# The prompt's cross attention, worked head by head between the chunk products of the query projection

## What is computed

```python
def cross_attend(xn, mk, mv, w_xq, w_xo):
    B, L = xn.shape[:2]
    q = (xn @ w_xq).reshape(B, L, N_X_HEADS, X_HEAD_DIM)
    s = jnp.einsum('bqhd,bkhd->bhqk', q, mk.astype(q.dtype)).astype(F32) * (X_HEAD_DIM ** -0.5)
    p = jax.nn.softmax(s, axis=-1).astype(q.dtype)
    o = jnp.einsum('bhqk,bkhd->bqhd', p, mv.astype(q.dtype))
    return o.reshape(B, L, X_WIDTH) @ w_xo
```

## Time and profile before

| | us |
|---|---|
| median of 3 runs | 1618.1 |
| lowest and highest | 1615.92, 1622.6 |
| the profiled execution | 1617.97 |
| its span | 1616.2 |

### The profile page before, as it was taken

How to read it: one execution, slowest core, us unless ns; L and a number is a source line. 1 busy time by engine, 2 the same in 40 slices (tenths; PEclk the granted TensorE clock), 3 DMA queues, 4 the chain that set the end, 5 groups by cost and what they waited for, 6 DMA issues and landing times.

```text
span 1616.2 us, 25068 instructions
## 1 busy us (share of the span) xinstructions
PE 1533.8 (95%) x9990; PEld 1474.5 (91%) x9990; DVE 647.3 (40%) x1187; ACT 444.2 (27%) x803; POOL 241.6 (15%) x269
## 2 busy tenths in 40 slices
PE   7999999888799899889999999999999999999997
PEld 6999888787699898778898999999999999999997
DVE  5544666454545421333356332233222432233322
ACT  6422444233221110332134320133111321033212
POOL 2100000232265300122442000000000000000143
PEclk9999999899599999999999999999999999999999
DMA  7553100102231211025542111111111111111112
GB/s 209 186 181 96 38 27 14 50 27 83 93 95 52 92 39 39 1 104 171 175 138 65 53 39 52 40 53 39 52 42 50 40 52 52 40 46 46 50 29 108
DMA packets 153774, 115.43 MB, mean 71 GB/s; under 512 B 13904, under 2 KB 143120, under 8 KB 153424
## 3 DMA queue, kind: packets, MB, share of 16 engines
q1 hardware_dynamic: 142160, 76.95, 16.5%
q0 software_dynamic: 9344, 33.20, 5.8%
q10 hardware_dynamic: 2192, 4.20, 0.8%
HBM read 101.19 MB, written 14.16 MB: 71 GB/s over the span
## 4 chain that ended last, share of the span: by engine, by line
PE 83%; issue 7%; DVE 4%; ACT 2%; DMA 2%; POOL 1%; SPq 0%; DVEq 0%; POOLq 0%; ACTq 0%
PE ps L353 24%; PE ps L354 23%; PE ps L355 23%; PE ps L1103 4%; PE ps L1423 2%; PE ps L1441 2%; DVE wlo L342 1%; PE ps L1191 1%; PE ps L1215 1%; ACT whi L326 1%; PE ps L1287 1%; DMA raw<-in_w_xv 1%; PE ps L1289 0%; DMA raw<-in_w_in 0%; DMA raw<-in_w_xk 0%
## 5 line engine op out<-in xcount | busy, mean ns | idle before, releaser
L353 PE MATMUL ps<-xhi,whi 128*128 128x352 f32 x1392 | 457.7, 329 | 14.1 <-DVE wlo L342 9.1
L354 PE MATMUL ps<-xlo,whi 128*128 128x352 f32 x1392 | 449.5, 323 | 0.0
L355 PE MATMUL ps<-xhi,wlo 128*128 128x352 f32 x1392 | 449.4, 323 | 0.0
L353 PE MATMUL ps<-yhi,whi 128*128 128x352 f32 x1152 | 374.1, 325 | 6.0 <-DVE wlo L342 2.1
L354 PE MATMUL ps<-ylo,whi 128*128 128x352 f32 x1152 | 370.1, 321 | 0.0
L355 PE MATMUL ps<-yhi,wlo 128*128 128x352 f32 x1152 | 369.9, 321 | 0.0
L353 PEld LDWEIGHTS ps<-xhi,whi 128*128 128x128 f32 x1392 | 264.4, 190 | 23.0 <-issue 15.1
L354 PEld LDWEIGHTS ps<-xlo,whi 128*128 128x128 f32 x1392 | 264.6, 190 | 0.1
L355 PEld LDWEIGHTS ps<-xhi,wlo 128*128 128x128 f32 x1392 | 263.8, 189 | 0.0
L326 ACT ACTIVATE whi<-raw 128x1024 fp32r<-128x1024 f32 x126 | 133.0, 1055 | 408.5 <-PE ps L355 364.4
L353 PEld LDWEIGHTS ps<-yhi,whi 128*128 128x128 f32 x1152 | 216.9, 188 | 8.6 <-DVE wlo L342 3.9
(11 more groups left out here) (263 smaller groups left out, 1343.8 us busy)
## 6 DMA issues: line engine op xcount, KB each, us to landing
raw<-in_w_up SPq DMA_DIRECT2D x32, 512.0 KB
raw<-in_w_down SPq DMA_DIRECT2D x32, 512.0 KB
raw<-in_w_xo SPq DMA_DIRECT2D x16, 512.0 KB
kx<-in_cache_mem_k POOLq DMA_DIRECT2D x16, 512.0 KB, 4.6
raw<-in_w_in SPq DMA_DIRECT2D x14, 512.0 KB, 3.8
spill<-hT POOLq DMA_DIRECT2D x8, 528.0 KB, 6.4
hT<-spill POOLq DMA_DIRECT2D x8, 528.0 KB, 5.7
xin<-in_x_prompt SPq DMA_DIRECT2D x8, 512.0 KB, 7.7
```

Of the source, the lines that this page charges most:

```text
L353: pe.matmul(out, whi[:, q, k, :], x1, start=k == 0, stop=False)
L354: pe.matmul(out, whi[:, q, k, :], x2, start=False, stop=False)
L355: mm = pe.matmul(out, wlo[:, q, k, :], x1, start=False, stop=k == KB - 1)
```

## The change

`stx` and its copies go: the scores take their stationary operand from `xq` itself. The attention is worked head by head. i = 8h + n is block n of head h (32 of them), j = 2h + half counts half heads of 512 tokens for the values (8 of them); the softmax goes by pairs of blocks (16 of them). Scores alternate between banks 2 and 3 by pairs. The values are 4 matmuls of 512 columns for each half head.

Units 0 and 1 of the query projection run as before. Then, for the heads 0 to 2, the six chunk products of the next two units stand with the pieces of the head between them: product, four scores; product, four times a turn and a score; product, values of the first half; product, four turns; product, values of the second half; product. The results of heads 0 to 2 are kept in `xq` over the used queries (`cross_keep`) and split into `yhi` and `ylo` later (`kept_hi`, `kept_lo`), since `yhi` and `ylo` are operands of the query projection until its end. Head 3 runs behind the last product. GpSimd's loads for the sample wait for the kept blocks now (`s_xol` 10 and 12), and the clearing of `qxm` stands behind them and waits for the last turn.

```diff
-            def x_stage(n2):
-                    pool.tensor_copy(stx[:, p], cols(xq, 0, KB, n)).then_inc(s_xst, 1)
...
+            pool.wait_ge(s_xol, 10)
             for b in range(2):
                 sx_load(pool, b, "cache_mem_k", 2 * b, lambda slot: s_kl[slot])
+            pool.wait_ge(s_xol, 12)
+            pool.wait_ge(s_xs, XSC)
             for b in range(2):
                 sx_load(pool, b, "cache_mem_v", values_at(b), lambda slot: s_kl[slot])
-            pool.wait_ge(s_xs, NQ)
+            pool.wait_ge(s_xpT, XSC)
             pool.memset(qxm[:], 0.0).then_inc(S("sx_q_kept"), 1)
```

ScalarE (`cross_exp` takes a pair of blocks, `cross_pT` half a head):

```diff
+            def cross_keep(j):
+                act.wait_ge(s_xo, j + 1)
+                copy(xq[:, j // 2 * 2 + 1, cross_half(j)], ps[:, cross_bank(j, 1), :]).then_inc(s_xoh, 1)
...
+            for h in range(XH - 1):
+                u = U_XQ + 2 + 2 * h
+                split_hi(act, u + 1, 1)
+                cross_exp(4 * h)
+                cross_exp(4 * h + 1)
+                cross_exp(4 * h + 2)
+                cross_pT(2 * h)
+                cross_exp(4 * h + 3)
+                split_hi(act, u + 2, 0)
+                cross_keep(2 * h)
+                cross_pT(2 * h + 1)
+                if h < XH - 2:
+                    cross_keep(2 * h + 1)
+            act.wait_ge(s_mm, chunks_before(U_XO))
+            for k in range(4):
+                kept_hi(k)
+            cross_keep(5)
+            cross_exp(12)
+            kept_hi(4)
+            cross_exp(13)
+            kept_hi(5)
+            cross_exp(14)
+            cross_pT(6)
+            cross_exp(15)
+            cross_hi(6, 0)
+            cross_pT(7)
+            cross_hi(6, 1)
+            cross_hi(7, 0)
+            cross_hi(7, 1)
```

TensorE:

```diff
+            def cross_values(j):
+                pe.wait_ge(s_xpe, j + 1)
...
+                for d in range(2):
+                    k = j // 2 * 2 + d
+                    for a in range(2):
+                        mm = pe.matmul(ps[:, cross_bank(j, d), :], mv[:, a, k * P:(k + 1) * P], xpT[:, a, cross_half(j)], start=a == 0, stop=a == 1)
+                mm.then_inc(s_xo, 1)
...
+            for h in range(XH - 1):
+                u, i = U_XQ + 2 + 2 * h, h * NQ
+                pe.wait_ge(s_wlo, u + 1)
+                product(pe, u, 0, 0, yhi, ylo, CW)
+                pe.wait_ge(s_ev, chunks_before(u))
+                for t in range(4):
+                    cross_scores(i + t)
+                product(pe, u, 0, 1, yhi, ylo, CW)
+                turns_and_scores(i)
+                product(pe, u, 0, 2, yhi, ylo, CW)
+                cross_values(2 * h)
+                pe.wait_ge(s_wlo, u + 2)
+                product(pe, u + 1, 1, 0, yhi, ylo, CW)
+                for t in range(4, NQ):
+                    cross_turn(i + t)
+                product(pe, u + 1, 1, 1, yhi, ylo, CW)
+                if h < XH - 2:
+                    cross_values(2 * h + 1)
+                product(pe, u + 1, 1, 2, yhi, ylo, CW)
+            cross_values(5)
+            pe.wait_ge(s_ev, chunks_before(U_XO))
+            i = 3 * NQ
+            for t in range(4):
+                cross_scores(i + t)
+            turns_and_scores(i)
+            cross_values(6)
+            for t in range(4, NQ):
+                cross_turn(i + t)
+            cross_values(7)
```

VectorE in the first three heads alternates the same way (`evacuate` of a chunk, maxima and scalings of two pairs, `cross_keep` of the other half of a result). Behind them:

```diff
+            kept_lo(0)
+            kept_lo(1)
+            cross_keep(5)
+            cross_max(12)
+            kept_lo(2)
+            cross_probs(12)
+            cross_max(13)
+            kept_lo(3)
+            cross_probs(13)
+            cross_max(14)
+            cross_probs(14)
+            cross_max(15)
+            cross_probs(15)
+            kept_lo(4)
+            kept_lo(5)
+            for j in (6, 7):
+                for d in range(2):
+                    cross_lo(j, d)
```

More of the change, by code:

```diff
@@ L962, in _ @@
             root(2)
[L963 to L988, removed]
+            split_hi(act, U_XQ + 1, 1)
+            split_hi(act, U_XQ + 2, 0)
+            def cross_exp(j):
+                act.wait_ge(s_xm, j + 1)
+                for i in (2 * j, 2 * j + 1):
+                    wait(act, s_xpT, i - NQ + 1)
+                    act.activation(xp[:, i % NQ, :], ps[:, 2 + j % 2, (i % 2) * NM:(i % 2) * NM + NM], ACT.Exp, scale=1.0 / 16, bias=wneg[:, i % NQ:i % NQ + 1],
+                                   accum_out=wsum[:, i % NQ:i % NQ + 1]).then_inc(s_xe, 1)
@@ new lines, in kept_hi @@
+            def kept_hi(k):
+                if k % 2 == 0:
+                    act.wait_ge(s_xol, (2, 4, 8)[k // 2])
+                else:
+                    act.wait_ge(s_xoh, (2, 4, 10)[k // 2])
+                copy(yhi[:, k, 0:TP], xq[:, k, 0:TP]).then_inc(s_xoh, 1)
+            for h in range(XH - 1):
[11 more added lines that the diff above has]
+                    cross_keep(2 * h + 1)
@@ L1411, in _ @@
             pe.wait_ge(s_lo, 2 * KB - 1)
-            units(U_XQ, 8, yhi, ylo, last_block=(s_lo, 2 * KB), before=lambda c: norm_sum(2) if c == 1 else None)
+            unit(pe, U_XQ, 0, yhi, ylo, last_block=(s_lo, 2 * KB), before=lambda c: norm_sum(2) if c == 1 else None)
+            unit(pe, U_XQ + 1, 1, yhi, ylo)
             pe.wait_ge(s_root, 3)
             pe.wait_ge(s_xld, 32)
[L1418 to L1423, removed]
-                mm.then_inc(s_xs, 1)
@@ L1426, in cross @@
[L1426 to L1432, removed]
-                    for a in range(2):
[L1434 to L1449, removed]
+            def cross_scores(i):
+                h, n = i // NQ, i % NQ
+                wait(pe, s_xe, i - 3)
+                for dd in range(2):
+                    mm = pe.matmul(ps[:, 2 + i // 2 % 2, (i % 2) * NM:(i % 2) * NM + NM], xq[:, 2 * h + dd, n * P:(n + 1) * P], mkT[:, 2 * h + dd, :], start=dd == 0, stop=dd == 1)
+                mm.then_inc(s_xs, 1)
@@ L1495, in _ @@
                     pe.wait_ge(s_wlo, u + 1)
+                if b == 0:
+                    pe.wait_ge(s_xol, XRES)
                 xo_product(u, c)
@@ L1517, in _ @@
             mm.then_inc(S("sx_o_turned"), 1)
-            pe.wait_ge(s_xol, NQ + 1)
+            pe.wait_ge(s_xol, XRES + 1)
             def xb(u):
@@ L1934, in cross_probs @@
[L1934 to L1950, removed]
+            evac(U_XQ, 0, scaled(xq, U_XQ), before=lambda c: invert(2, c))
+            evac(U_XQ + 1, 1, scaled(xq, U_XQ))
+            def cross_max(j):
+                c0, m = j % 4 * 2, slice(j % 2 * 2, j % 2 * 2 + 2)
+                dve.wait_ge(s_xs, 2 * j + 2)
+                st.did(dve.tensor_reduce(wmax[:, m], ps[:, 2 + j % 2, :].rearrange("p (t c) -> p t c", t=2), AX.X, ALU.max))
+                st.settle()
+                dve.tensor_scalar(wneg[:, c0:c0 + 2], wmax[:, m], -1.0 / 16, None, ALU.mult).then_inc(s_xm, 1)
@@ new lines, in kept_lo @@
+            def kept_lo(k):
+                dve.wait_ge(s_xoh, (6, 7, 8, 9, 11, 12)[k])
+                dve.tensor_tensor(ylo[:, k, 0:TP], xq[:, k, 0:TP], yhi[:, k, 0:TP].bitcast(F32), ALU.subtract).then_inc(s_xol, 1)
+            for h in range(XH - 1):
+                u, j = U_XQ + 2 + 2 * h, 4 * h
+                split_lo(dve, u + 1, 1)
+                evacuate(u, 0, 0, scaled(xq, U_XQ))
+                cross_max(j)
+                cross_max(j + 1)
+                cross_probs(j)
+                cross_probs(j + 1)
+                evacuate(u, 0, 1, scaled(xq, U_XQ))
+                cross_max(j + 2)
+                cross_probs(j + 2)
+                cross_max(j + 3)
+                cross_probs(j + 3)
+                evacuate(u, 0, 2, scaled(xq, U_XQ))
+                split_lo(dve, u + 2, 0)
+                cross_keep(2 * h)
+                evacuate(u + 1, 1, 0, scaled(xq, U_XQ))
+                evacuate(u + 1, 1, 1, scaled(xq, U_XQ))
+                if h < XH - 2:
+                    cross_keep(2 * h + 1)
+                evacuate(u + 1, 1, 2, scaled(xq, U_XQ))
```

57 lines of the change are left out of this document (40 added, 17 removed).

## The result

The changed kernel takes 1594.87 us (median of 4 runs, 1591.6 to 1598.62) against 1617.01 us of the kernel before in the same comparison (4 runs, 1615.89 to 1622.6). The ratio is 0.9857, with a 95% interval of 0.9824 to 0.989: 1.4% faster. A later comparison of the same two kernels (6 and 11 runs) gave 0.9862, 0.9839 to 0.9885. Forecast were 1598.9 us, with a range from 1594 to 1608.

What follows compares the result with a forecast made beforehand. TensorE was taken to bound the kernel (83% of the chain). Three heads 45.9 us plus last head 24.8 make 70.7 against 88.39, 17.7 less; with 1.4 behind it, 19.1 off 1617.97 gives 1598.9 us, range 1594 to 1608.

Steps and rivals of the forecast that it cites:

- the change-over: Heads 0 to 2: each of 14 pieces between two products costs about 0.19 us, 2.7 us in all; bounds 0 and 5.6.
- the clock: Prompt's cross attention: 4.6 us of low clock go, and 1.4 us more are gained behind the sample's first turn.
- What bounds the kernel: TensorE carries the chain; the 88.39 us stretch holds 65.5 of net products, about 18.3 of waiting, 4.6 of lower clock.
- Staging: Ahead of the first scores: GpSimd's eight copies into stx go, and with them their 2.7 us wait; the others were hidden.
- Values: Value products, 128 matmuls become 32 of 512 columns: 3.41 us each of eight pieces, gain 3.4 us; bounds 0 and 3.4.
- Waits under the products: Heads 0 to 2: products cover softmax, copies and weight splits, costed at nothing; without cover 1 to 3 us a piece.
- The last head: Last product's end to the sample's first turn: 18.9 us products, 5.3 waits, about 0.6 matmul ends, 24.8; bounds 20 and 30.
- Rivals 1 and 2: Last head: waits passing 1.9 us drop the clock, about 1604 us (0.21); or all at half clock, 1617.8 (0.06).
- The rule of the Trainium skill: Against the last head: frequent micro-idles between matmul groups let the clock swing between two levels; transposes do not count as activity.
- the bound of 1.9 us: Last head: the wait length beyond which rival 1 has TensorE's clock drop, each drop costing 1.4 to 2.8 us.

Runs made afterwards that it cites:

- the third experiment: The kernel before, with scores reading the queries in place instead of GpSimd's staged copies: 1616.41 us, ratio 0.999 to the kernel before.
- the first experiment: The changed kernel with each value product of 512 columns cut into four of 128: 1595.1 us, ratio 0.9859 to the kernel before.
- the seventh kernel: The changed kernel with two more VectorE reductions ahead of the first scaling of each of heads 0 to 2: 1594.22 us, one run.
- the eighth: The changed kernel with five more VectorE reductions ahead of the first scaling of each of heads 0 to 2: 1610.28 us, one run.
- fourth: The changed kernel with GpSimd's clearing and filling of qxm ahead of its value loads for the sample: 1596.38 us, ratio 0.9868 to the kernel before.
- sixth: The changed kernel with three more VectorE reductions ahead of the last head's first scaling: 1604.8 us, one run.
- ninth: The changed kernel with value groups cut to fill the last head's waits, ScalarE and VectorE lists reordered, qxm cleared early: 1592.0 us, ratio 0.984 to the kernel before.
- the second: The changed kernel with units 2 to 7 of the query projection run first, the pieces of heads 0 to 2 behind them: 1606.76 us, ratio 0.9936.
- fifth: The changed kernel with one more VectorE reduction ahead of the last head's first scaling: 1597.31 us, one run.

## Why the prediction was right or wrong, and what its terms were

The step that failed is the change-over: 14 pieces between products were put at 2.7 us and cost 0.6 in the trace. One reason failed too, that wide value matmuls save 3.4 us; they save about 1. The stage, the waits and the clock came as forecast.

*What bounds the kernel* was right: the stretch of 88.39 us held the time, and its waits and its low clock went. Only the split of it was a little off: 65.5 us of net products counts a value group at 3.84, which from start to start is 3.67.

*Staging*: right, 0.7 us instead of 2.7 ahead of the first scores, shown by the third experiment, and with it the low clock in the first group.

*Values*: the size of a new group was right (3.43 measured, 3.41 forecast), the reason was not. The forecast gain of 3.4 us from width is about 1 us in the first experiment; it set the length of a record (3.84) against a distance from start to start (3.46). The sum did not suffer, since the new stage was added up from the scores' distance and not by subtracting from the old groups. That the size came out is luck as far as the reason goes.

*The change-over* is the mis-sized term, and the largest part of the gap. "A piece put between two products costs about 0.19 us": 14 of them were put at 2.7 us. Measured, the projection with 14 pieces grows by 135.80 - 92.0 = 43.8 us (92.0 is from the first product behind the norm, 546.32, to 638.31), and the pieces' own time is 43.2 by the forecast's sizes, so 0.6 us remain, 0.05 a piece. Even that may be no change-over, since products with nothing between them also take 3.86 us in the second and third head (607.76 to 611.62) and not 3.82; why stays open. A product between pieces does take 4.06 us to the next piece's start, as the row has it (4.01). But the piece ahead of it gives 0.19 back: its scores pass TensorE on 3.27 us behind their start and not 3.46. I read one side of the boundary only, and the lower bound of this term, 0, was nearly the truth: this is the case that the range's lower edge stood for.

*Waits under the products*: none, right, with 2.3 us of slack against 2.4 reckoned; with 2.3 us of added work a head no wait shows (the seventh kernel), with 5.7 one of 3.20 (the eighth).

*The last head*: 24.8 forecast, 23.9 measured. Its waits were 1.1, 0.7, 1.1, 1.1, 1.3 in the forecast and 0.91, 0.32, 0.70, 1.12, 0.91 in the trace, in the same places and for the reasons given, the GpSimd queue at its end included. They are shorter at least in part since an instruction of VectorE starts ahead of its predecessor's recorded end (`kept_lo(2)` at 687.79, where the record before it runs from 687.71 to 687.88), so its chains add up to less than the sum of their records.

*The clock*: 1.00 in the last head, right, and 1.8 us were gained behind the sample's first turn, for which 1.4 stood. Rivals 1 and 2 did not occur. The rule of the Trainium skill that spoke against it ("TensorE: Matmul & The Clock Gate", "A second HAM failure mode: psum-queue depth-cycling") is not borne out in this stretch: five waits in 24 us, turns between them, and a granted clock of 1.00.

Together: 2.1 us of change-over, 0.9 of the last head and 0.4 behind it are the 3.4 us by which the traces' 22.5 us (20.7 up to the sample's first turn, 1.8 behind it) exceed the 19.1 forecast. The rest, 1.3 us in unchanged code and 0.3 ahead of the stage, is the execution's: the 1.3 are the clock behind the wait of 2.21 us at the start of the MLP.

## What to carry to other kernels

Build the new stage bottom-up from start-to-start distances, not from record lengths: a TensorE record includes the end of its last matmul, which the next group overlaps (3.84 us against 3.67 for the old values), and a boundary has two sides that must be read together. Independent matmul work of one product's length between two steps of a softmax chain hides the chain as long as it lasts longer than the chain does; the slack is read off as the distance between "ready" and "asked for", and it can be used or measured by adding work to it. What is left behind the last product is worth ordering by hand too: cutting two groups that were already there into halves filled three of the five waits, and clearing `qxm` ahead of the loads took a fourth.

## What the runs showed of the hardware that was not expected

A wait of one length drops TensorE's clock in some executions and not in others. The wait in the first unit of the query projection is the same in every kernel here, 1.91 to 1.95 us. In eight traces (the kernel before, the changed one twice, the first, fourth, sixth, eighth and ninth) the clock is at 0.50 behind it for about 3 us; in four (the second, third, fifth and seventh) it stays at 1.00. The window of one microsecond behind the wait, in the changed kernel:

```profile
557.00:558.00 1.00, 1.00 (x5) 1.00 (x5) 1.00 (x1) 0.00 (x0) 0.00 (x0) 0.50 0.00 0
```

The same place in the seventh kernel, whose added reductions come later than it:

```profile
559.00:560.00 1.00, 1.00 (x9) 1.00 (x8) 1.00 (x1) 0.00 (x0) 0.00 (x0) 1.00 0.00 0
```

That moves a run by about 1.6 us (1.3 to 1.7 for one drop, by the sixth and eighth kernel) with the same instructions ahead of it. Other places of the twelve traces behave alike. A wait of 2.33 us near 336 us is followed by a low clock in seven traces and by a full one in five, the one of 2.21 us at the start of the MLP in six and six, and one of 1.45 us near the end of the kernel in five and seven. Why the clock falls in one execution and not in the other stays open.

It also says that the bound of 1.9 us in the prediction is none, on either side: a wait of 1.98 us in the last head and some of 2.33 left the clock alone, and some of 1.45 did not. Only behind waits of 2.5 us and more was it low each time, the wait for the first input at the very start of the kernel apart. A comparison of two traces should therefore first set the places side by side where the clock fell: here it is 1.3 us of the 24.1 between the two spans.
